# Low parts of 26 weight slabs moved from GpSimd to VectorE in a three-layer forward pass

## The chip, the cores and the metric

One core of one Trainium2 chip runs the whole program in one launch. The metric is the device time of one execution in microseconds (us); a kernel is compared by the median of its runs. The profile is that of one execution.

## The reference

256 tokens of width 1024 go through three blocks, all in float32. Cut to what matters:

```
def first_block(x, ...):                     # two layers
    for layer in range(2):
        xn = rms_norm(x, norm_mix[layer])
        x = x + (even_mixer if layer == 0 else odd_mixer)(xn, ...)
        x = x + square(relu(rms_norm(x, norm_mlp[layer]) @ w1)) @ w2     # 1024 -> 4096 -> 1024
    return rms_norm(x, norm_final)

def second_block(x, mem, ...):               # one layer
    proj = rms_norm(x) @ w_in                # 12 + 12 slabs of 256 columns
    xa, ga, qm, km, vm, qx, g_logits = split(proj)
    xa  = causal_dwconv(xa, 4 taps)
    y_a = rg_lru(xa, ...) * gelu(ga)         # gates: xa @ w_a, xa @ w_x per head, then a scan
    y_b = moba_attention(qm, km, vm)         # causal, with ALiBi slopes
    y_c = memory_cross_attention(qx, mem)
    merged = sum(sigmoid(g_logits)[n] * (y[n] @ w_branch[n]) for n in range(3))
    x = x + merged @ w_out
    h = rms_norm(x)
    x = x + (gelu(causal_dwconv(h @ w_gate, 3 taps)) * (h @ w_up)) @ w_down
    return rms_norm(x)
```

## The kernel before

Each product is made in three matmuls of a lower precision: a weight W is split into a high part `whi` (W rounded) and a low part `wlo` = W - `whi`, and so is the activation (`XH` and `XL`, `HH` and `HL`, `OH` and `OL`, `GH` and `GL`). TensorE adds high x high, low x high and high x low (line 498, `product`).

**Slabs.** `weight_plan` lists the weights as 192 slabs in the order of use, nearly all of 128 x 2048 elements (1 MB). SyncE loads slab n into one of five `raw` buffers (line 2069) when slab n - 5 has been used. ScalarE makes the high part (`high`, line 918), into one of three `whi` buffers, so it waits until TensorE has finished the slab three before. The low part is one subtraction, `wlo = raw - whi`, which waits for the high part; it is VectorE's (`low`, line 1300) or GpSimd's (`low`, line 1952). `pooled(n)` says which, and each engine goes over all slabs and skips those of the other. The numbers of the slabs that matter here: 18 to 33 `w1` and 34 to 49 `w2` of the first MLP, 86 to 89 `od_o` (the output of the second mixer), 90 to 105 `w1` and 106 to 121 `w2` of the second MLP, 122 to 133 `in2` (the third mixer's inputs), 134 to 151 twelve `gate` and six `branch` slabs in the order of `BLEND`, 152 to 155 `out2`, then `fg` and `fu` in turn.

**Order of work.** Each engine has its own program, written out by hand, and works in its order; semaphores tie them. On every engine `ahead(n)` stands where slab n is used and makes the part of slab n + 2. So a low part that VectorE makes stands in its queue in front of what it does with the product of slab n: `scaled` (line 1727) copies it out of PSUM with the norm's factor, `onto` (line 1417) and `onto_natural` (line 1424) add it to the residual `XT`, `down` (lines 1434 and 1436) does so at the end of an MLP.

**The stages of the change.** After a residual add, ScalarE makes `XH` (line 950) and VectorE `XL` (line 1334), both from SBUF; TensorE's next slab takes them chunk by chunk. GpSimd adds up the squares of the norm (line 1962). In the third mixer the first slabs feed a convolution on VectorE, `conv` (lines 1751 and 1755), and its result the LRU gates on TensorE, `lru_gate` (line 819), which stands behind slabs 126 and 127. When the LRU's scan (line 1785) is done, GpSimd loads the ALiBi distances over the gates' buffer (line 2033) and makes each head's bias (`slope`, line 2041), which the maxima of the attention need (line 1368). A step of the attention then has maxima on VectorE, exponentials on ScalarE (line 980), normalizing on VectorE (line 1383), transposes on TensorE (line 608), copies, values (line 635); between the steps stand the gate and branch slabs. `branch` multiplies by the gates and adds (lines 1833 and 1835), ScalarE and VectorE split the sum into `GH` (line 1214) and `GL` (line 1839), and `out2` takes it.

Of the kernel before, what the change touches and what calls it, by code (L numbers as in the profile page):

```python
# [265 lines left out]
def build(nc, A, out):  # L266
    with ExitStack() as ctx:
# [62 lines left out]
        plan = weight_plan(A)  # L330
# [46 lines left out]

        def pooled(n):

            name = plan[n][0]  # L380
            if name == "w1":
                return plan[n - 3][0] != "w1"
            if name == "branch":
                return sum(p[0] == "branch" for p in plan[:n]) > 1
            return name in ("out2", "in2", "fg")

        def ahead_of(n):

# [903 lines left out]
        def vector(dve):  # L1292
            once = Once(dve)

            def low(n):
                if not split(n) or pooled(n):
                    return
                once.wait_ge(*at(("raw", n)))
                once.wait_ge(*at(("whi", n)))
                dve.tensor_tensor(wlo_of(n), raw_of(n), f32(whi_of(n)), ALU.subtract).then_inc(*tell(s_wlo, ("wlo", n)))  # L1300
# [643 lines left out]
        def gpsimd(pool):  # L1944
            once = Once(pool)

            def low(n):
                if not split(n) or not pooled(n):
                    return
                once.wait_ge(*at(("raw", n)))  # L1950
                once.wait_ge(*at(("whi", n)))
                pool.tensor_tensor(wlo_of(n), raw_of(n), f32(whi_of(n)), ALU.subtract).then_inc(*tell(s_pool_wlo, ("wlo", n)))  # L1952
# [216 lines left out]
```

## Time and profile before

| | us |
|---|---|
| median of 3 runs (1332.22 to 1334.56) | 1334.36 |
| profiled execution | 1332.44 |
| its span, first to last instruction | 1330.6 |
| TensorE busy | 1265.6 |
| VectorE busy | 834.4 |
| ScalarE busy | 621.2 |
| GpSimd busy | 263.9 |

The mean granted clock of TensorE is 0.980. In the rows, PE is TensorE (PEld its weight loads), DVE VectorE, ACT ScalarE, POOL GpSimd; L918 is line 918. A row of a timeline has the start in us from the span's start, the time in us, engine, line, operation, output<-inputs, shapes and the number of instructions in the row; in brackets stands how long the engine was idle before it and what released it.

### The profile page before, as it was taken

Reading aid. Unit: us, or ns where it says so; the run is one execution under the profiler, and the core shown is the slowest. Engines: PE = TensorE matmul, PEld = TensorE weight load, DVE = VectorE, ACT = ScalarE, POOL = GpSimd, SP = SyncE. Lnnn points to the kernel's source line nnn. Section 1 sums busy time; section 2 is a strip of 40 time slices with the busy share of each in tenths; the row PEclk is TensorE's granted clock in tenths of the full one; section 3 lists DMA queues with packets and bytes.
Section 4 is the critical chain, followed back from the end, with each engine's and each line's share of the span. In section 5 each row is a group of like instructions: output and inputs, shape, how many; then the busy total and the mean of one; then the engine's idle time right before and its main releaser. Section 6 shows DMA issues by size and latency. Waiting matters only on the chain.

```text
span 1330.6 us, 23858 instructions
## 1 busy us (share of the span) xinstructions
PE 1265.6 (95%) x10309; PEld 1219.8 (92%) x10309; DVE 834.4 (63%) x1108; ACT 621.2 (47%) x761; POOL 263.9 (20%) x103
## 2 busy tenths in 40 slices
PE   7989999999999999998789999989999898999997
PEld 7967889999999999997689999989989888999997
DVE  6667556655565666666756655584777676555653
ACT  5554455544345445444355543435366445444431
POOL 2300130000012111110230000376211364433000
PEclk9999989999999999999989999999999998999998
DMA  9532345555566554544246555643543344555550
GB/s 253 171 127 88 104 137 182 190 188 179 176 224 200 183 179 156 189 156 131 65 127 190 189 176 177 196 159 127 174 149 127 127 159 135 183 190 188 176 176 32
DMA packets 194710, 213.99 MB, mean 161 GB/s; under 512 B 5235, under 2 KB 182718, under 8 KB 194606
## 3 DMA queue, kind: packets, MB, share of 16 engines
q1 hardware_dynamic: 189518, 204.93, 47.7%
q10 hardware_dynamic: 4896, 7.08, 1.8%
q8 instruction: 81, 1.33, 0.4%
q0 software_dynamic: 192, 0.46, 0.1%
q14 instruction: 23, 0.19, 0.0%
HBM read 205.11 MB, written 1.05 MB: 155 GB/s over the span
## 4 chain that ended last, share of the span: by engine, by line
PE 74%; DVE 9%; ACT 7%; issue 5%; POOL 1%; DMA 1%; ACTq 0%; DVEq 0%; POOLq 0%
PE ps L498 67%; ACT whi L918 3%; PE ps L600 2%; PE ps L635 2%; PE ps L608 1%; DVE XL L1334 1%; DVE BIG L1755 1%; ACT SN L980 1%; POOL wlo L1952 1%; DVE XT L1424 1%; DVE XT L1417 1%; DVE BIG L1835 1%; DVE SN L1368 1%; DVE BIG L1751 1%; ACT XH L950 1%
## 5 line engine op out<-in xcount | busy, mean ns | idle before, releaser
L498 PE MATMUL ps<-XH,whi 128*128 128x256 f32 x1704 | 489.0, 288 | 9.3 <-ACT XH L950 9.3
L1300 DVE TENSOR_TENSOR wlo<-raw,whi 128x2048 fp32r<-128x2048 f32 (+1 forms) x151 | 352.6, 2336 | 231.2 <-ACT whi L918 231.0
L498 PE MATMUL ps<-XL,whi 128*128 128x256 f32 x1704 | 485.1, 286 | 2.3 <-DVE XL L1334 1.6
L498 PE MATMUL ps<-XH,wlo 128*128 128x256 f32 x1704 | 483.3, 285 | 0.0
L918 ACT ACTIVATE whi<-raw 128x2048 fp32r<-128x2048 f32 (+1 forms) x189 | 359.5, 1903 | 182.9 <-PE ps L498 156.3
L498 PEld LDWEIGHTS ps<-XH,whi 128*128 128x128 f32 x1704 | 329.7, 194 | 15.4 <-ACT XH L950 11.5
L498 PEld LDWEIGHTS ps<-XL,whi 128*128 128x128 f32 x1704 | 329.2, 194 | 4.3 <-DVE XL L1334 2.9
L498 PEld LDWEIGHTS ps<-XH,wlo 128*128 128x128 f32 x1704 | 329.8, 194 | 0.2
L1952 POOL TENSOR_TENSOR wlo<-raw,whi 128x2048 fp32r<-128x2048 f32 x38 | 176.3, 4645 | 484.6 <-ACT whi L918 484.6
L498 PE MATMUL ps<-HH,whi 128*128 128x256 f32 x832 | 229.5, 283 | 0.0
L498 PE MATMUL ps<-HL,whi 128*128 128x256 f32 x832 | 229.3, 283 | 0.0
L498 PE MATMUL ps<-HH,wlo 128*128 128x256 f32 x800 | 226.5, 283 | 2.3 <-POOL wlo L1952 2.3
L498 PEld LDWEIGHTS ps<-HH,whi 128*128 128x128 f32 x832 | 157.5, 192 | 0.0
L498 PEld LDWEIGHTS ps<-HL,whi 128*128 128x128 f32 x832 | 157.5, 192 | 0.0
L498 PEld LDWEIGHTS ps<-HH,wlo 128*128 128x128 f32 x800 | 153.6, 192 | 2.5 <-POOL wlo L1952 2.5
L2013 POOL TENSOR_TENSOR TB<-TB,BIG 128x512 f32<-128x512 f32 x24 | 42.0, 1751 | 384.1 <-DMA TB<-TA 384.1
L980 ACT ACTIVATE SN<-SN,stat 128x512 f32<-128x512 f32 (+2 forms) x64 | 38.4, 600 | 141.8 <-DVE stat L1368 141.7
L498 PE MATMUL ps<-whi,XH 128*128 128x256 f32 x256 | 73.1, 285 | 0.0
L498 PE MATMUL ps<-whi,XL 128*128 128x256 f32 x256 | 72.4, 283 | 0.0
L498 PE MATMUL ps<-wlo,XH 128*128 128x256 f32 x256 | 72.4, 283 | 0.0
L608 PE MATMUL ps<-ident,SN 128*128 128x128 f32 x232 | 38.6, 290 | 20.5 <-DVE SN L1383 20.4
L498 PE MATMUL ps<-OH,whi 128*128 128x256 f32 x192 | 56.1, 292 | 1.6 <-ACT SN L980 1.6
(224 smaller groups left out, 1512.3 us busy)
## 6 DMA issues: line engine op xcount, KB each, us to landing
raw<-in_mlp_w_dram SPq DMA_DIRECT2D x64, 1024.0 KB, 5.3
raw<-in_od_w_in_dram SPq DMA_DIRECT2D x36, 1024.0 KB, 5.3
raw<-in_w_in_dram SPq DMA_DIRECT2D x24, 1024.0 KB, 5.2
raw<-in_w_ffn_gate_dram SPq DMA_DIRECT2D x12, 1024.0 KB, 5.1
raw<-in_w_ffn_up_dram SPq DMA_DIRECT2D x12, 1024.0 KB, 5.1
raw<-in_w_ffn_down_dram SPq DMA_DIRECT2D x12, 1024.0 KB, 5.1
raw<-in_ev_w_in_dram SPq DMA_DIRECT2D x6, 1024.0 KB, 12.1
TB<-TA ACTq DMA_DIRECT2D x96, 64.0 KB, 4.2
```

What stands on the lines that cost most here:

```text
L498: m = pe.matmul(to, l[c][a], r[c][b], start=first and k == 0, stop=last and k == 3 * n - 1)
L600: m = pe.matmul(banks[u][:, lo:hi], l, r, start=start, stop=stop)
L608: m = pe.transpose(b[:, to:to + P], SN[:, u % 3, of:of + P], ident[:, :])
L635: m = pe.matmul(b[p0:p0 + n, a:z], v, PT[:, u % 3, lo:hi], start=start, stop=stop)
L918: act.activation(whi_of(n), raw_of(n), ACT.Copy, scale=1.0).then_inc(*tell(s_whi, ("whi", n)))
L950: act.activation(XH[:, c, :], XT[:, c, :], ACT.Copy, scale=g).then_inc(*tell(s_xhi, ("xhi", stage, c)))
L980: m = act.activation(SN[:, u % 3, lo:hi], src[:, lo:hi], ACT.Exp, bias=stat[:, u % 3, k:k + 1], scale=-1.0 if biased else 1.0, accum_out=s ...
L1300: dve.tensor_tensor(wlo_of(n), raw_of(n), f32(whi_of(n)), ALU.subtract).then_inc(*tell(s_wlo, ("wlo", n)))
L1334: dve.scalar_tensor_tensor(out=XL[:, c, :], in0=XT[:, c, :], scalar=g, in1=f32(XH[:, c, :]), op0=ALU.mult, op1=ALU.subtract).then_inc(*tel ...
L1368: m = dve.tensor_tensor_reduce(out=SN[:, u % 3, lo:hi], in0=b[:, lo:hi], in1=bias(lo), scale=-0.125 if kind == DIL else -1.0, scalar=3e38, ...
L1952: pool.tensor_tensor(wlo_of(n), raw_of(n), f32(whi_of(n)), ALU.subtract).then_inc(*tell(s_pool_wlo, ("wlo", n)))
L2013: pool.tensor_tensor(z, z, twice(RP[:, S:512]), ALU.mult).then_inc(*tell(s_pool, ("sine", k)))
```

## The change

`pooled(n)` gave GpSimd the low parts of 38 slabs: the first three `w1` slabs of either MLP (18 to 20, 90 to 92), all twelve `in2` slabs, the last four of the six `branch` slabs (146, 149, 150, 151), the four `out2` slabs and the twelve `fg` slabs. Now it gives it the twelve `fg` slabs alone. The other 26 are made by VectorE, with the same subtraction, each at the place in its queue where `ahead` stands. Nothing else is changed.

```diff
         def pooled(n):
 
-            name = plan[n][0]
-            if name == "w1":
-                return plan[n - 3][0] != "w1"
-            if name == "branch":
-                return sum(p[0] == "branch" for p in plan[:n]) > 1
-            return name in ("out2", "in2", "fg")
+            return plan[n][0] == "fg"
 
         def ahead_of(n):
```

## Rows read from the trace of the kernel before

**Rows 1.** The page's engine table: busy us, share of the span, instructions.

```profile
PE 1265.6 (95%) x10309; PEld 1219.8 (92%) x10309; DVE 834.4 (63%) x1108; ACT 621.2 (47%) x761; POOL 263.9 (20%) x103
```

**Rows 2.** Windows: length, busy us by engine, granted clock, DMA share, GB/s.

```profile
869.00:910.00 41.00, 36.27 (x280) 32.70 (x280) 34.08 (x36) 14.26 (x15) 25.25 (x6) 0.92 0.38 123
...
950.00:1046.00 96.00, 92.15 (x764) 87.60 (x760) 67.91 (x116) 53.06 (x83) 18.38 (x11) 1.00 0.44 145
...
1090.00:1118.00 28.00, 21.82 (x155) 21.04 (x156) 14.66 (x17) 12.13 (x17) 18.77 (x7) 0.88 0.36 116
```

**Rows 3.** The low parts by line: ns min/median/max, first and last start, forms.

```profile
L1952 POOL TENSOR_TENSOR wlo<-raw,whi x38: 4543/4622/5073, 161.3 to 1228.8; 128x2048 fp32r<-128x2048 f32 x38
...
L1300 DVE TENSOR_TENSOR wlo<-raw,whi x151: 2265/2292/4321, 16.5 to 1306.0; 128x2048 fp32r<-128x2048 f32 x150, 128x1280 fp32r<-128x1280 f32 x1
```

**Rows 4.** Two lines of VectorE, the second with an input in PSUM.

```profile
L1334 DVE SCALAR_TENSOR_TENSOR XL<-XT,V,XH x32: 472/480/4901, 9.0 to 1111.5; 128x256 fp32r<-128x256 f32 x32
...
L1727 DVE SCALAR_TENSOR_TENSOR BIG<-ps,RS x22: 678/683/693, 874.2 to 1058.4; 128x512 f32<-128x512 f32 x22
```

**Rows 5.** Timeline of GpSimd at the mixer's input.

```profile
873.81 14.22 POOL L1952 TENSOR_TENSOR wlo<-raw,whi 128x2048 fp32r<-128x2048 f32 x3 [3.22 <-ACT whi L918]
```

**Rows 6.** Timeline of VectorE there.

```profile
856.55 3.62 DVE L1436 TENSOR_TENSOR XT<-XT,TA 128x256 f32<-128x256 f32 x1
...
875.70 3.08 DVE L1751 TENSOR_SCALAR BIG<-BIG,V 128x256 f32<-128x256 f32 x1
878.81 10.01 DVE L1755 SCALAR_TENSOR_TENSOR BIG<-BIG,V 128x255 f32<-128x255 f32 x3
...
895.94 1.52 DVE L1755 SCALAR_TENSOR_TENSOR BIG<-BIG,V 128x255 f32<-128x255 f32 x3
```

**Rows 7.** Timelines ahead of the first MLP, GpSimd and VectorE.

```profile
168.75 4.61 POOL L1952 TENSOR_TENSOR wlo<-raw,whi 128x2048 fp32r<-128x2048 f32 x1 [2.86 <-ACT whi L918]
...
169.79 4.25 DVE L1334 SCALAR_TENSOR_TENSOR XL<-XT,V,XH 128x256 fp32r<-128x256 f32 x2 [0.65 <-ACT XH L950]
```

**Rows 8.** Timelines ahead of the second MLP, VectorE and GpSimd.

```profile
647.83 1.14 DVE L1424 TENSOR_TENSOR XT<-XT,ps 128x256 f32<-128x256 f32 x2 [0.46 <-PE ps L498]
...
651.30 2.56 DVE L1383 TENSOR_SCALAR SN<-SN,stat 128x512 f32<-128x512 f32 x1
...
663.62 3.95 DVE L1334 SCALAR_TENSOR_TENSOR XL<-XT,V,XH 128x256 fp32r<-128x256 f32 x2 [0.65 <-ACT XH L950]
...
648.98 4.59 POOL L1952 TENSOR_TENSOR wlo<-raw,whi 128x2048 fp32r<-128x2048 f32 x1 [35.92 <-ACT whi L918]
```

**Rows 9.** The LRU gates by line, columns as in rows 3.

```profile
L819 PE MATMUL ps<-BIG,SN x32: 376/376/685, 892.3 to 908.9; 64*64 64x256 f32 x32
```

**Rows 10.** The chain that ended last, behind the first gate: start, us, what.

```profile
900.51 6.87 PE ps L498 x48
907.39 1.87 PE ps L819 x16
909.26 5.96 PE ps L498 x48
```

**Rows 11.** The same chain ahead of the attention.

```profile
951.74 4.17 DMA BIG<-in_c_alibi_dram
```

**Rows 12.** Timelines of the mixer's end, VectorE, TensorE and ScalarE.

```profile
1042.63 4.81 DVE L1835 TENSOR_TENSOR BIG<-BIG,TB 128x512 f32<-128x512 f32 x1
...
1073.93 0.68 DVE L1833 TENSOR_TENSOR TB<-ps,BIG 128x512 f32<-128x512 f32 x1
...
1076.72 0.68 DVE L1833 TENSOR_TENSOR TB<-ps,BIG 128x512 f32<-128x512 f32 x1
...
1085.87 5.73 DVE L1417 TENSOR_TENSOR XT<-XT,ps 128x512 f32<-128x512 f32 x8
...
1049.64 1.09 PE L608 MATMUL ps<-ident,SN 128*128 128x128 f32 x4 [3.99 <-DVE SN L1383]
...
1110.53 0.91 ACT L950 ACTIVATE XH<-XT,V 128x256 fp32r<-128x256 f32 x2 [0.70 <-DVE XT L1417]
```

## The prediction

> **What bounds the kernel now.** I read the page's engine table first: TensorE is busy for 1265.6 of 1330.6 us [rows 1]. At most 65 us can be won, and only where TensorE waits. So I read the windows of the stages that the 38 GpSimd low parts stand in. TensorE idles for 4.7 us of 869 to 910, 3.9 us of 950 to 1046 and 6.2 us of 1090 to 1118, and its granted clock is 0.92 and 0.88 in the first and the last, 1.00 between [rows 2]. The MLPs and the GLU behind have no such gaps.
>
> Then I read the low parts by line. One takes 4.62 us on GpSimd and 2.29 us on VectorE [rows 3]. GpSimd's own speed is hardly waited for. What matters is what its instruction does to VectorE: an XL of L1334 takes 0.48 us as a rule and up to 4.90 us, while L1727, which reads PSUM, stays within 678 to 693 ns [rows 4]. In the timelines GpSimd works from 873.81 to 888.03 without a pause [rows 5], and in that time VectorE's convolution, all in SBUF, takes 3.08 us for an instruction of 0.40 and 10.01 us for three that need 1.52 later [rows 6]. I read this as: of the two engines' instructions that have all their data in SBUF, one runs at a time, and the other engine's waits for its end.
>
> **First MLP (slabs 18 to 20): 0.9 us won.** On VectorE low 18 runs while it would idle, and low 20 while it waits for the norm's sums. Low 19 stands in front of the last residual adds. Its high part ends at 168.6, just before GpSimd starts at 168.75 [rows 7], so VectorE holds it from 168.65 to 170.9, then add 0.7, high half 0.5 behind it, two XL 0.9: done at 173.1. Now the two XL are blocked until 174.0 [rows 7].
>
> **Second MLP (90 to 92): 0.4 us lost.** Low 90 comes in front of the adds of `od_o`: until 651.2 (high part done by 648.9, when GpSimd starts), where four adds now begin at 647.8. With 0.8 us of waits absorbed and the 2.1 us block at 651.30 gone (2.56 against 0.49), the last heads run 0.8 us later. Low 91 delays the residual adds by 3.1 us more and saves the 3.95 - 0.88 = 3.1 us block and some hand-over, about 0.4 back [rows 8]. Low 92 lies in the wait for sums. Bounds: 0.4 won to 1.0 lost.
>
> **Mixer input (122 to 133): 0.6 + 7.3 us won.** One of the MLP's last two `down` adds is blocked by low 123 now (3.62 us at 856.55 instead of 0.42 [rows 6]); low 123 on VectorE delays it by 1.4 us, less than that. So TensorE's 0.6 us wait for the last XH goes. Then I place VectorE's queue from the factors' end (873.9): low 125 2.2, slab 0.6, two convolutions of 1.9 (0.40 + 1.52, as at 895.94) [rows 6], low 126, slab, two convolutions. The four are ready at 887.9. TensorE reaches the first LRU gate at 892.3 - 0.6 = 891.7, so it doesn't wait. Before, the gate's 16 matmuls lasted from 892.3 [rows 9] to 900.5, and the second gate's, with nothing to wait for, 1.87 us; the slab between them took 6.87 us instead of 5.9 [rows 10]. That is 8.2 - 1.9 = 6.3 us and 1.0 us: 7.3. The other low parts (127 to 133) come 1.7 us or more ahead of TensorE in the same placing, the tightest being 133 (ready 928.8, wanted 930.5). Between them VectorE does the ratios unblocked.
>
> **Attention of the mixer: 3.5 us won.** GpSimd starts the alibi load at 951.74, when the scan is done; it lands 4.2 us later, and the first slope follows [rows 11]. In my placing the scan is done at 939.9: the load starts 11.5 us earlier, and with it the chain of maxima, exponentials, high part, low part. TensorE is only 7.9 us earlier, so its waits here, 3.85 us of which 0.35 belong to the wait that ends at 1049.64, go [rows 2, 12]. Low 146 costs nothing: ScalarE's gates and their two table loads last longer than it.
>
> **Branches and output slab (149 to 155): 5.2 us won.** I count from the end of the last gate slab before the last transposes, 1045.65 (1049.64 - 3.99); call it A. The 3.99 us wait goes: it stands behind a branch add that took 4.81 instead of 0.69 [rows 12]. Then TensorE: transposes and values 1.1, slabs 148 and 149 11.7, values 0.7, four slabs of 5.8. Slab 153 ends at A + 36.7 and frees the buffer of high part 156, which is done at A + 38.7; GpSimd, which keeps `fg`, starts low 156 at A + 38.8. VectorE: low 152 at A + 16.1 (ScalarE must first copy the last attention output) to 18.3; two merges of 2.79 (1073.93 to 1076.72) [rows 12] to 23.9; 1.1 of waiting for high part 153; low 153 to 27.3; two merges to 32.9; 1.1 of waiting; low 154 from 34.0 to 36.2; four residual adds of 0.72 (8 in 5.73) [rows 12]; low 155 at A + 39.1. GpSimd is 0.3 us ahead. So low 155 is held until 43.4 and ends at 45.7, where TensorE wanted it at 42.4. Behind it: four adds 2.9, two residual blocks of 2.1, ScalarE's high part and low 157 to 56.9, one block more, one add. The last high half starts at A + 59.7. Now it starts at 1110.53, which is A + 64.9 [rows 12]: 5.2 us. The FFN and all after it are TensorE without gaps, so this stays won to the end.
>
> **Rule against row.** The Trainium skill's page Perfetto Trace Analysis, section Optimizing Scalar/DVE Operations, says that shifting work between VectorE and GpSimd may not help, since they share a read port. By that rule alone the 26 low parts would only change who waits, and the sum would be near 0 (1332.4). The rows say that the one keeps the other out for 4.62 us and the other needs 2.29 us for the same work [rows 3], so I keep the sum. The page SBUF — State Buffer, section SBUF: two separate sides, says that the pair belongs to whichever instruction starts first, for all of it; the blocked XL [rows 4, 7] agree, and by that rule too 0.3 us decide on 4 us at slab 155.
>
> **Sum.** -0.9 + 0.4 - 0.6 - 7.3 - 3.5 - 5.2 = -17.1 us. VectorE gets 26 x 2.29 = 59.5 us more, GpSimd 120 us less. The profiled execution took 1332.4 us, so 1315.3; the median of the runs is 1.9 us above it, by which it is 1317.3. I say 1316.5.
>
> **Rivals.**
> - VectorE first at slab 155 (0.27): 0.3 us in a chain of twenty instructions is little. Then low 155 ends at A + 41.4, GpSimd waits, and the end of the tail comes 4.1 us earlier: 21.2 us won, 1311.2 to 1313.1.
> - The alibi load held (0.12): it is issued from GpSimd, just as VectorE runs low 136. If its start or its writing waits for VectorE's low parts, all that follows slips: two low parts are 4.6 us, 1320; at worst all of the 11.5 us, 1326.8. Against it: low 136 stood behind the scan before too, and the load took 4.17 us [rows 11]. The skill's page SBUF — State Buffer has a warning of this kind on loads from GpSimd's queue; no row here shows one.
> - Slower (0.05): VectorE's long instructions are not GpSimd's doing. Then the blocks stay and low parts come on top, in its queue ahead of what TensorE waits for: 124 to 127 before the convolutions (9.2 us), 152 to 155 before the residual (9.2), 19, 90 and 91 (6.9, less 4 hidden): about 1354. It decides once XL and convolution keep over half of their extra time with GpSimd idle. Against it: 0.48 us is their median [rows 4].
> - No change (0.06): TensorE's waits turn up elsewhere, in loads of weights or a lower clock, and 1332 to 1336 stays. Against it: the DMA share is 0.38 and 0.44 where the waits are [rows 2].
> - The forecast has 0.50.
>
> Chances: faster 0.50 + 0.27 + 0.12 = 0.89, same 0.06, slower 0.05, with 0.2% (2.7 us) as the bound, about what a measurement of this kernel can tell. The range goes from 1309 (VectorE first, the second MLP at its better bound) to 1327 (the alibi load at worst), and leaves out the last two cases.
>
> **What would show it.** L1952 has 12 instructions and L1300 177; nearly all L1334, L1751 and L1755 take 0.4 to 0.5 us; the LRU gate has no wait on L1755; the alibi load starts 11 to 12 us earlier; low 155 takes either 2.3 us or over 6. I am wrong if VectorE's durations don't fall, if a wait on L1300 of more than 4 us appears at TensorE, or if the mixer's attention starts early and TensorE isn't earlier at its end.

## The result and the profile after

| | before | after |
|---|---|---|
| median of 4 runs each, us | 1334.46 (1332.22 to 1336.17) | 1315.44 (1314.61 to 1317.58) |
| ratio, 95% interval | | 0.9861 (0.9841 to 0.9880) |
| profiled execution, us | 1332.44 | 1317.58 |
| its span, us | 1330.6 | 1315.8 |

The kernel is 19 us faster on the medians; the two profiled executions lie 14.9 us apart. Lines of the changed kernel have numbers smaller by 5: L1300 is now L1295, L498 L493, L819 L814, L1334 L1329.

The page's engine table of the changed kernel. TensorE's busy time is 2.5 us below what it was [rows 1]; VectorE took over 26 low parts, 59.5 us of work, and its busy time rose by 7 us only. The rest had been time in which its instructions stood still.

```profile
PE 1263.1 (96%) x10309; PEld 1221.5 (93%) x10309; DVE 841.5 (64%) x1134; ACT 621.6 (47%) x761; POOL 144.6 (11%) x77
```

The changed kernel by line, columns as in [rows 3]. Twelve low parts are left on GpSimd. No XL takes over 486 ns (up to 4901 before [rows 4]), and the convolution's two lines take 0.40 and 0.48 us everywhere. One low part on VectorE takes 6.5 us.

```profile
L1947 POOL TENSOR_TENSOR wlo<-raw,whi x12: 4562/4626/4630, 1075.0 to 1214.9; 128x2048 fp32r<-128x2048 f32 x12
...
L1295 DVE TENSOR_TENSOR wlo<-raw,whi x177: 2265/2292/6535, 16.3 to 1292.1; 128x2048 fp32r<-128x2048 f32 x176, 128x1280 fp32r<-128x1280 f32 x1
...
L1329 DVE SCALAR_TENSOR_TENSOR XL<-XT,V,XH x32: 475/480/486, 9.2 to 1096.8; 128x256 fp32r<-128x256 f32 x32
...
L1746 DVE TENSOR_SCALAR BIG<-BIG,V x4: 402/405/409, 880.0 to 888.5; 128x256 f32<-128x256 f32 x4
...
L1750 DVE SCALAR_TENSOR_TENSOR BIG<-BIG,V x12: 482/483/485, 880.5 to 889.9; 128x255 f32<-128x255 f32 x4, 128x254 f32<-128x254 f32 x4, 128x253 f32<-128x253 f32 x4
```

Windows of the changed kernel, columns as in [rows 2]. The first row, the end of the second mixer, is taken up further below. The mixer's input and its attention have no gap left at TensorE (4.7 and 3.9 us before [rows 2]). The residual of the tail, the last row, has 7.8 us of gaps, and a mean granted clock of 0.82, a mixture of the two levels, 1.2 and 2.4 GHz, behind TensorE's waits.

```profile
625.00:660.00 35.00, 25.79 (x216) 22.51 (x216) 26.33 (x59) 12.36 (x24) 0.00 (x0) 0.87 0.20 61
869.00:912.00 43.00, 43.00 (x355) 40.95 (x355) 33.81 (x44) 18.92 (x23) 0.00 (x0) 1.00 0.47 152
944.00:1040.00 96.00, 96.00 (x798) 91.84 (x797) 65.98 (x124) 55.48 (x85) 9.48 (x8) 1.00 0.47 153
1075.00:1104.00 29.00, 21.20 (x142) 20.11 (x141) 18.14 (x20) 10.69 (x16) 13.01 (x5) 0.82 0.32 105
```

The timeline of VectorE at the mixer's input: low 125 and the convolution behind it. Three instructions that took 10.01 us [rows 6] take 1.52.

```profile
877.23 2.28 DVE L1295 TENSOR_TENSOR wlo<-raw,whi 128x2048 fp32r<-128x2048 f32 x1
879.42 0.68 DVE L1722 SCALAR_TENSOR_TENSOR BIG<-ps,RS 128x512 f32<-128x512 f32 x1
880.03 0.40 DVE L1746 TENSOR_SCALAR BIG<-BIG,V 128x256 f32<-128x256 f32 x1
880.46 1.52 DVE L1750 SCALAR_TENSOR_TENSOR BIG<-BIG,V 128x255 f32<-128x255 f32 x3
```

The chain of the changed kernel there. Both LRU gates take 1.9 us, the slab between them 5.9, as the forecast had it.

```profile
894.05 1.88 PE ps L814 x16
895.93 5.94 PE ps L493 x48
901.87 1.87 PE ps L814 x16
903.74 8.34 PE ps L493 x68
```

Timelines of the changed kernel: GpSimd's alibi load and first slope, then low 155 and 156 (VectorE, GpSimd) and TensorE's waits behind them. The load starts 9.8 us earlier than at [rows 11]. GpSimd starts low 156 at 1075.03, VectorE reaches low 155 at 1075.26, 0.23 us too late; 6.54 is 4.4 us of standing and 2.2 of work. The two starts lie 0.23 to 0.24 us apart in each of the five traces with this order of work.

```profile
941.90 0.58 POOL L2028 DMA_DIRECT2D BIG<-in_c_alibi_dram  x1 [77.13 <-DVE BIG L1780]
944.83 3.46 POOL L2036 TENSOR_SCALAR TB<-BIG 128x384 f32<-128x384 f32 x3 [2.35 <-DMA BIG<-in_c_alibi_dram]
...
1075.26 6.54 DVE L1295 TENSOR_TENSOR wlo<-raw,whi 128x2048 fp32r<-128x2048 f32 x1
...
1075.03 4.62 POOL L1947 TENSOR_TENSOR wlo<-raw,whi 128x2048 fp32r<-128x2048 f32 x1 [91.68 <-ACT whi L913]
...
1081.85 0.39 PE L493 MATMUL ps<-HH,wlo 128*128 128x256 f32 x1 [2.60 <-DVE wlo L1295]
1094.27 0.58 PE L493 MATMUL ps<-XH,whi 128*128 128x256 f32 x1 [4.88 <-ACT XH L945]
1096.39 0.58 PE L493 MATMUL ps<-XH,whi 128*128 128x256 f32 x1 [0.31 <-ACT XH L945]
```

### The profile page after: what moved, and what is told of

Read it like the earlier page. It is cut to its first block, busy times and chain, and to the rows that moved or that the text cites. A ratio compares the mean times of both kernels' runs of the same rounds, so it can differ in the third digit from the quotient of the medians.

```text
span 1315.8 us, 23857 instructions
## 1 busy us (share of the span) xinstructions
PE 1263.1 (96%) x10309; PEld 1221.5 (93%) x10309; DVE 841.5 (64%) x1134; ACT 621.6 (47%) x761; POOL 144.6 (11%) x77
## 3 DMA queue, kind: packets, MB, share of 16 engines
HBM read 205.11 MB, written 1.05 MB: 157 GB/s over the span
## 4 chain that ended last, share of the span: by engine, by line
PE 84%; DVE 6%; ACT 3%; issue 3%; DMA 0%; ACTq 0%; POOL 0%; DVEq 0%
PE ps L493 76%; PE ps L595 2%; PE ps L630 2%; PE ps L603 2%; ACT whi L913 2%; DVE XT L1419 1%; DVE XT L1412 1%; DVE wlo L1295 1%; DVE XL L1329 1%; DVE SN L1363 1%; PE ps L529 1%; ACT XH L945 0%; ACT SN L975 0%; DMA TB<-TA 0%; PE ps L814 0%
## 5 line engine op out<-in xcount | busy, mean ns | idle before, releaser
L1295 DVE TENSOR_TENSOR wlo<-raw,whi 128x2048 fp32r<-128x2048 f32 (+1 forms) x177 | 417.1, 2357 | 260.5 <-ACT whi L913 260.3
L493 PE MATMUL ps<-XH,whi 128*128 128x256 f32 x1704 | 489.0, 288 | 10.4 <-ACT XH L945 10.4
L493 PE MATMUL ps<-XL,whi 128*128 128x256 f32 x1704 | 485.5, 286 | 0.8 <-DVE XL L1336 0.4
L493 PE MATMUL ps<-XH,wlo 128*128 128x256 f32 x1704 | 483.9, 285 | 0.0
L493 PEld LDWEIGHTS ps<-XH,whi 128*128 128x128 f32 x1704 | 330.2, 194 | 15.4 <-ACT XH L945 12.2
L493 PEld LDWEIGHTS ps<-XL,whi 128*128 128x128 f32 x1704 | 329.9, 194 | 2.6 <-DVE XL L1329 1.2
L493 PEld LDWEIGHTS ps<-XH,wlo 128*128 128x128 f32 x1704 | 330.3, 194 | 0.1
L493 PE MATMUL ps<-HH,whi 128*128 128x256 f32 x832 | 229.6, 284 | 0.2 <-DVE XT L1412 0.2
L493 PE MATMUL ps<-HL,whi 128*128 128x256 f32 x832 | 229.3, 283 | 0.0
L493 PE MATMUL ps<-HH,wlo 128*128 128x256 f32 x800 | 226.5, 283 | 2.6 <-DVE wlo L1295 2.6
L493 PEld LDWEIGHTS ps<-HH,whi 128*128 128x128 f32 x832 | 157.5, 192 | 0.4 <-DVE XT L1412 0.4
L493 PEld LDWEIGHTS ps<-HL,whi 128*128 128x128 f32 x832 | 157.5, 192 | 0.0
L493 PEld LDWEIGHTS ps<-HH,wlo 128*128 128x128 f32 x800 | 153.6, 192 | 2.8 <-DVE wlo L1295 2.8
L1947 POOL TENSOR_TENSOR wlo<-raw,whi 128x2048 fp32r<-128x2048 f32 x12 | 55.4, 4620 | 161.8 <-ACT whi L913 161.8
L493 PE MATMUL ps<-whi,XH 128*128 128x256 f32 x256 | 73.1, 285 | 0.0
L493 PE MATMUL ps<-whi,XL 128*128 128x256 f32 x256 | 72.4, 283 | 0.0
L493 PE MATMUL ps<-wlo,XH 128*128 128x256 f32 x256 | 72.4, 283 | 0.0
L493 PE MATMUL ps<-OH,whi 128*128 128x256 f32 x192 | 57.3, 299 | 2.8 <-ACT SN L975 2.0
L493 PE MATMUL ps<-OL,whi 128*128 128x256 f32 x192 | 55.4, 288 | 0.0
```

The source lines that it names most:

```text
L493: m = pe.matmul(to, l[c][a], r[c][b], start=first and k == 0, stop=last and k == 3 * n - 1)
```

## The experiments

The theory, **blocks**: of VectorE's and GpSimd's instructions with all data in SBUF one runs at a time, so GpSimd's low part of 4.62 us holds up what VectorE has next. The rival, **late weights**: TensorE waited for the low parts themselves, which GpSimd makes slowly. Each group below was compared on one chip with common runs of the kernel before (its median is given).

### One part of the change at a time (before: 1335.78 us, 22 runs)

**Mixer input alone**

```diff
-            return name in ("out2", "in2", "fg")
+            return name in ("out2", "fg")          # the tests for w1 and branch stay
```

> Only the twelve in2 slabs (122 to 133) on VectorE, the rest as before. Theory of the blocks (a GpSimd instruction on SBUF keeps VectorE's instructions on SBUF waiting, and their lateness is what TensorE waits for): the LRU gate's waits go and the alibi load starts 11 to 12 us earlier, so 0.6 + 7.3 + 3.5 = 11.4 us faster than before, about 1323; the 4 us wait behind the branch add at the mixer's end stays. Rival, the late weights (GpSimd's 4.6 us make the low parts late): no wait of TensorE on GpSimd's low part stands there, so no change, 1334.

1319.02 us (4 runs), ratio 0.9875 (0.9856 to 0.9895): 16.8 us won where 11.4 was forecast, most of the whole. The LRU gates wait no more. The profiled execution is 13.0 us below that of before, and one wait of the attention is left, TensorE's timeline in this kernel:

```profile
1036.47 0.88 PE L608 MATMUL ps<-ident,SN 128*128 128x128 f32 x4 [2.11 <-DVE SN L1383]
```

It took 3.99 us before [rows 12]: with the chain of the attention earlier, half of that wait goes without the branch slabs being moved. The forecast had left it whole; the other part of the 5 us too much is not accounted for.

**Branch and output slabs alone**

```diff
-            if name == "branch":
-                return sum(p[0] == "branch" for p in plan[:n]) > 1
-            return name in ("out2", "in2", "fg")
+            return name in ("in2", "fg")           # the test for w1 stays
```

> Only the four branch slabs (146, 149 to 151) and the four out2 slabs on VectorE. Blocks: 5.2 us faster than before, about 1329, the 4 us wait before the last transposes gone. Late weights: only the 2.3 us wait on GpSimd's low part of slab 154 goes, about 1332.

1328.76 us (11 runs), ratio 0.9958 (0.9941 to 0.9974): 7.0 us won on the medians, 3.5 to 7.9 by the interval. That holds the 5.2 us of blocks and not the 2.3 us of late weights. TensorE's timeline still shows the LRU gate's waits on the convolution, with in2's low parts on GpSimd:

```profile
895.14 0.65 PE L817 MATMUL ps<-BIG,SN 64*64 64x256 f32 x4 [2.14 <-DVE BIG L1753]
897.70 1.12 PE L817 MATMUL ps<-BIG,SN 64*64 64x256 f32 x4 [1.92 <-DVE BIG L1753]
```

**MLP slabs alone**

```diff
-            if name == "w1":
-                return plan[n - 3][0] != "w1"      # the rest stays
```

> Only the six w1 slabs (18 to 20, 90 to 92) on VectorE. Prediction's terms: 0.9 won and 0.4 lost, 1334. If what the profile after shows at the second MLP (3.5 us later than the same stretch of before) is the work of low 90 and 91 in VectorE's queue, 2.5 to 3 us slower, about 1337; if it is the granted clock of that one execution, 1334. Late weights: 1334.

1335.50 us (12 runs), ratio 0.9998 (0.9987 to 1.0008): nothing. Six of the 26 moves are worth nothing together, which is near the sum of the forecast's two terms (-0.9 and +0.4); the trace of this kernel says more on them below. The three parts add up to 24.1 us, the whole won 19.0 above and 17.5 below. About 1.9 us of the last wait of the attention count in the first two parts both. The rest of the difference is not accounted for; the collision of the low parts 155 and 156 is no reason, since the branch and output slabs alone have it too (low 155 starts at 1086.26, 0.23 us behind low 156, and takes 6.54 us).

**The blocks put back.** The changed kernel, with GpSimd subtracting constants into idle tiles when the high part of each in2 slab is done. Nothing waits for these results.

```diff
                 if not pooled(n):
+                    if plan[n][0] == "in2":
+                        once.wait_ge(*at(("whi", n)))
+                        if n > 123:
+                            once.wait_ge(*at(("dummy", n - 2)))
+                        pool.tensor_tensor(<OH or OL, idle here, 128x2048>,
+                                           <ident, broadcast>, <ones, broadcast>, ALU.subtract)
+                            .then_inc(*tell(s_pool, ("dummy", n)))
                     return
```

> The changed kernel, and GpSimd does twelve subtractions of the same size (128 x 2048, constants into the idle OH and OL) at the times of its former low parts of the in2 slabs; nothing waits for their results. Blocks: the waits of TensorE at the LRU gate are back, and longer than in the kernel before by about 4.5 us, since VectorE has two low parts more in that queue: 11 to 16 us slower than the changed kernel, 1327 to 1332. Late weights: VectorE's low parts are as early as in the changed kernel and so is the end, 1315.

1350.32 us (6 runs), ratio 1.0104 (1.0087 to 1.0121): 14.5 us above the kernel before and 34 to 35 above the medians of the changed kernel, for twelve instructions on an engine that had nothing to do. Late weights fall here: GpSimd makes none of these weights, and the time was to stay at 1315. The sign is that of blocks; the size and the place were wrong. The LRU gate does not wait in this trace; TensorE waits 3.93 us for XH and 3.04, 11.03 and 5.61 us for low parts that VectorE makes late. I had priced the convolution only. Timelines of this kernel (VectorE, GpSimd, TensorE):

```profile
887.15 5.99 DVE L1295 TENSOR_TENSOR wlo<-raw,whi 128x2048 fp32r<-128x2048 f32 x1
...
897.76 9.84 DVE L1750 SCALAR_TENSOR_TENSOR BIG<-BIG,V 128x255 f32<-128x255 f32 x3
...
890.92 6.65 POOL L1950 TENSOR_TENSOR OH<-ident,ones 128x2048 fp32r<-128x2048 f32 x1
...
893.19 0.39 PE L493 MATMUL ps<-XH,wlo 128*128 128x256 f32 x1 [3.04 <-DVE wlo L1295]
...
911.74 0.58 PE L493 MATMUL ps<-XH,wlo 128*128 128x256 f32 x1 [11.03 <-DVE wlo L1295]
...
957.76 0.58 PE L493 MATMUL ps<-wlo,XH 128*128 128x256 f32 x1 [5.61 <-DVE wlo L1295]
```

With long instructions on both engines each pays for the other: low parts on VectorE take up to 6.76 us, GpSimd's instruction takes 6.65 us behind one of them, and three instructions of the convolution take 9.84 again. So now TensorE does wait for low parts, those of VectorE.

### Order, load and length (before: 1334.21 us, 11 runs)

**The changed kernel again**

> The changed kernel once more, beside the others of this call: 1315.4, 19 to 20 us faster than before.

1316.74 us (5 runs), ratio 0.9855 (0.9835 to 0.9875): 17.5 us below the kernel before, a little less than said.

**Low 155 first.** The changed kernel, with VectorE's low 155 ahead of the residual adds of slab 152:

```diff
             for k in range(2):
                 ahead(OUT2 + k)
+            for k in range(2):
                 for j in range(4):
                     onto(OUT2 + k, j, j)
```

> The changed kernel with low 155 ahead of the residual adds of slab 152 in VectorE's queue, so that it starts 2.9 us earlier, before GpSimd's low 156 can. Blocks (who starts first holds the other off): low 155 takes 2.3 us, TensorE's 2.6 us wait for it goes, the residual chain ends 4.1 us earlier: 1311.3. Rival, the residual chain hangs on something else there: TensorE waits as long, but on XH, 1315.4.

1310.50 us (4 runs), ratio 0.9821 (0.9802 to 0.9840): 6.2 us below the changed kernel on the medians, and its slowest run is faster than the fastest of the other. VectorE's timeline there, then TensorE's:

```profile
1069.84 2.28 DVE L1295 TENSOR_TENSOR wlo<-raw,whi 128x2048 fp32r<-128x2048 f32 x1
1072.04 6.45 DVE L1412 TENSOR_TENSOR XT<-XT,ps 128x512 f32<-128x512 f32 x9
...
1072.78 0.39 PE L493 MATMUL ps<-HH,whi 128*128 128x256 f32 x1 [2.39 <-DVE XT L1412]
1087.86 0.39 PE L493 MATMUL ps<-XH,whi 128*128 128x256 f32 x1 [0.39 <-ACT XH L945]
```

Low 155 takes 2.28 us and the nine adds, which read PSUM, run beside GpSimd's low 156 (1072.48 to 1077.08) at their usual 0.72 us. TensorE's four waits of the tail of over 0.1 us, 7.98 us, become three of 3.54. The 2.60 us wait for low 155 does not simply go, as expected: TensorE now waits 2.39 us for the adds, which stand behind low 155. What goes is most of the 4.88 us wait for XH, of which 0.39 is left.

**The alibi load held back.** The changed kernel, with a wait of GpSimd for the product of the second gate slab ahead of the load:

```diff
             once.wait_ge(*at("lru h"))
+            once.wait_ge(*at(("product", "slab", BLENDS + 1)))
             pool.dma_start(alibi, A["c_alibi"])
```

> The changed kernel, with GpSimd's alibi load held until TensorE has finished gate slab 135, some 9 us later than in the changed kernel and at the time it had before. The prediction's step (attention runs on the VectorE and ScalarE chain that the load starts): TensorE waits for the normalized scores again, 5 to 8 us slower than the changed kernel, about 1322. Rival, TensorE's slabs bound the attention and the load's time is covered: 1315.4.

1325.21 us (6 runs), ratio 0.9938 (0.9917 to 0.9959): 8.5 us above the changed kernel, where 5 to 8 was forecast. Timelines, GpSimd and TensorE:

```profile
947.06 0.58 POOL L2029 DMA_DIRECT2D BIG<-in_c_alibi_dram  x1 [86.88 <-PE ps L493]
952.52 3.46 POOL L2037 TENSOR_SCALAR TB<-BIG 128x384 f32<-128x384 f32 x3 [4.88 <-DMA BIG<-in_c_alibi_dram]
...
961.87 0.90 PE L603 MATMUL ps<-ident,SN 128*128 128x128 f32 x3 [8.78 <-DVE SN L1378]
```

The load is issued 5.2 us later than in the changed kernel, not 9, and takes 2.5 us longer to land. A slope that comes 7.7 us later is one wait of 8.78 us. The time of this load is what the attention hangs on.

**Shorter holds.** The kernel before, all 38 low parts on GpSimd still, each in four instructions of 128x512:

```diff
-                pool.tensor_tensor(wlo_of(n), raw_of(n), f32(whi_of(n)), ALU.subtract).then_inc(*tell(s_pool_wlo, ("wlo", n)))
+                w, r, h = wlo_of(n), raw_of(n), f32(whi_of(n))
+                for s in <the four quarters of the slab>:
+                    m = pool.tensor_tensor(w[s], r[s], h[s], ALU.subtract)
+                m.then_inc(*tell(s_pool_wlo, ("wlo", n)))
```

> The kernel before, all 38 low parts on GpSimd as there, each as four instructions of a quarter (128 x 512) in place of one. Blocks: VectorE gets in after 1.2 us at most, not 4.6, so its blocks at the XL, the branch adds and the normalizing shrink to a quarter, those of the convolution by less, because GpSimd's next quarter follows at once: 3 to 9 us faster than before, about 1329. Late weights: the low parts take 4.6 us or more as before, no gain or slower, 1335 to 1337.

1313.72 us (6 runs), ratio 0.9849 (0.9826 to 0.9872): as much as the change itself. The theory's side is right, its size too low by 15 us. The quarters by line, GpSimd's timeline at the mixer's input, VectorE's convolution beside it, and TensorE at the LRU gate:

```profile
L1956 POOL TENSOR_TENSOR wlo<-raw,whi x152: 1259/1297/1747, 159.6 to 1210.9; 128x512 fp32r<-128x512 f32 x152
...
870.69 22.22 POOL L1956 TENSOR_TENSOR wlo<-raw,whi 128x512 fp32r<-128x512 f32 x16 [3.02 <-ACT whi L918]
...
872.36 1.23 DVE L1751 TENSOR_SCALAR BIG<-BIG,V 128x256 f32<-128x256 f32 x1
873.63 4.26 DVE L1755 SCALAR_TENSOR_TENSOR BIG<-BIG,V 128x255 f32<-128x255 f32 x3
...
893.76 1.04 PE L819 MATMUL ps<-BIG,SN 64*64 64x256 f32 x4 [3.32 <-DVE BIG L1755]
```

The low parts are made no faster (four quarters take 5.2 us, one whole 4.62), so late weights fall a second time. VectorE gets one instruction in after each quarter: 1.42 us each where it was 3.3 [rows 6]. GpSimd is busier than before, 288.7 us, and the kernel is 20 us faster.

### The collision at the tail, and the length again (before: 1334.05 us, 11 runs)

**All low parts on VectorE**, with low 155 first:

```diff
-            return plan[n][0] == "fg"
+            return False
```

> VectorE makes all low parts, the twelve of fg too, with low 155 ahead of the residual adds of slab 152; GpSimd only adds up squares. By the theory (one engine's all-SBUF instruction keeps the other's out), GpSimd can hold nothing up any more, but low 156 now stands in VectorE's queue in the residual chain, where it costs its own 2.3 us: 1312 to 1314, 2 us above the kernel with the order changed alone (1310.5). If VectorE becomes the bound in the FFN (twelve times 2.3 us more in some 185 us, of which it is busy for 111): 1320 or more.

1313.19 us (4 runs), ratio 0.9843 (0.9822 to 0.9864): the time that the theory gave, 2.7 us above low 155 first alone, though the two intervals overlap. The twelve more low parts do not make VectorE the bound (861.9 us busy); the residual chain pays for low 156 in one longer wait at TensorE, 3.69 us where it was 0.39:

```profile
1088.20 0.58 PE L493 MATMUL ps<-XH,whi 128*128 128x256 f32 x1 [3.69 <-ACT XH L945]
```

**Low 155 first, fg's low parts in quarters.** The diffs of the two kernels above, together.

> The kernel with the order changed (low 155 ahead of the residual adds of slab 152), with GpSimd's twelve low parts of fg made in four instructions each. By the theory nothing that TensorE waits for is held by GpSimd any more, so the quarters have nothing left to win: 1310.5 as without them, within 1.5 us. If quarters win by something other than shorter holds (GpSimd itself faster, for instance): 1307 or less.

1312.97 us (5 runs), ratio 0.9827 (0.9805 to 0.9849). The median is 2.5 us above the 1310.5, outside the 1.5 us that I gave; against the ratio of 0.9821 of low 155 first alone the intervals overlap, so no difference is shown. Quarters win nothing where nothing that TensorE waits for is held.

**Halves.** The kernel before, with each low part in two instructions of 128x1024.

> The kernel before, with each of GpSimd's low parts made in two instructions of 128x1024 instead of one of 128x2048. If the loss goes with the length of one hold (4.6 us whole, 1.26 us in quarters, about 2.4 us in halves), about half to two thirds of what the quarters won is won here: 1321 to 1325. If any gap between GpSimd's instructions is enough, since VectorE has one waiting instruction at a time: 1314 to 1317, like the quarters.

1322.78 us (6 runs), ratio 0.9914 (0.9889 to 0.9939): 11 of the quarters' 20 us. The loss goes with the length of a hold; a gap alone is not enough. The line of the low parts, then TensorE's waits at the LRU gate and at the end of the attention:

```profile
L1956 POOL TENSOR_TENSOR wlo<-raw,whi x76: 2343/2407/2867, 158.8 to 1223.0; 128x1024 fp32r<-128x1024 f32 x76
...
895.00 0.65 PE L819 MATMUL ps<-BIG,SN 64*64 64x256 f32 x4 [1.35 <-DVE BIG L1755]
...
1045.08 1.09 PE L608 MATMUL ps<-ident,SN 128*128 128x128 f32 x4 [2.35 <-DVE SN L1383]
```

## Why the prediction was right

The steps between marks of the two profiled executions, after against before:

| mark | after - before, us | step, measured | step, forecast |
|---|---|---|---|
| first LRU gate starts (894.0, 892.3) | +1.7 | +1.7 | -1.1 |
| slab behind the second gate starts (903.74, 909.26) | -5.5 | -7.2 | -7.3 |
| end of the last gate slab, A (1036.22, 1045.65) | -9.4 | -3.9 | -3.5 |
| last high half at TensorE (1096.39, 1111.09) | -14.7 | -5.3 | -5.2 |
| end of the span (1315.8, 1330.6) | -14.8 | -0.1 | 0 |

- **The mechanism** held where TensorE hung on it: taken away in one part (mixer input, output), put back without the weights (34 to 35 us lost), and made shorter (halves, quarters). By the Trainium skill, page SBUF — State Buffer, section SBUF: two separate sides, whichever instruction starts first keeps the pair for all of it; the 0.23 us at low 155 and the quarters agree, the slopes (below) do not. The page Perfetto Trace Analysis of the Trainium skill, section Optimizing Scalar/DVE Operations, says that moving work between the two might not help, since they share a read port. That they get in each other's way is what the rows show; that the sum would be near 0 for it is not: the move gave 19 us.
- **Its wording was too wide.** What the traces show held are VectorE's `tensor_tensor`, `scalar_tensor_tensor` and `tensor_scalar` with all data in SBUF. A reciprocal, all in SBUF too, is not held: in the kernel before, the one at 924.57 lies inside GpSimd's first low part (924.44 to 929.07) and takes 3.35 us, as the one at 934.41 does with GpSimd idle (VectorE, then GpSimd):

```profile
924.57 3.35 DVE L1770 RECIPROCAL TA<-TA 128x512 f32<-128x512 f32 x1
...
934.41 3.35 DVE L1770 RECIPROCAL TA<-TA 128x512 f32<-128x512 f32 x1
...
924.44 9.65 POOL L1952 TENSOR_TENSOR wlo<-raw,whi 128x2048 fp32r<-128x2048 f32 x2 [0.20 <-ACT whi L918]
```

Nor does every GpSimd instruction hold to its end: beside a slope, a `tensor_scalar` of 1.20 us, VectorE's first normalizing takes 0.55 us for 0.29 and the second its usual 0.34, and both end before the slope does (five times in the kernel before; the profile's spans of GpSimd are rough). On this form the rows do not bear out the rule that the Trainium skill gives, and the rows decide. So look at the pair of instructions, not only at where their data lie.

- **Mixer input and attention.** The gates run without a wait, the alibi load comes 9.8 us earlier and TensorE has no gap from 944 to 1040. I had the load 11.5 us earlier; the difference is the 2.8 us lost ahead of the gates (below), less 1 us; so the 11 to 12 us that was to show it did not come. From issue to landing it took 2.9 us, by the view of DMA issues, where [rows 11] had 4.2. The rival with the load held did not come: low 136 ran on VectorE from 941.52 to 943.8, over the issue, and the load was there at 944.8.
- **Tail.** GpSimd was ahead by 0.23 us where I had 0.3, low 155 stood, TensorE waited 2.60 us for it, and the step came out as 5.3 for 5.2. A margin of 0.3 us at the end of a chain of twenty placed instructions came out partly by luck, though in the five traces it comes out the same. The rival, VectorE first, was priced at 4.1 us less and a median of 1313.1; the experiment that puts low 155 first won 6.2 us.
- **MLPs: the mis-sized term.** -0.9 + 0.4 - 0.6 was to be -1.1 at the first gate and was +1.7: -0.8 stood there ahead of the first moved instruction, +0.2 came from the first MLP, +3.5 from the second and -1.1 behind it (rounded). Ahead of the first MLP the last XH came 0.9 us earlier as placed, but TensorE's next 30 matmuls took 6.34 us in place of 5.20, at a granted clock of 0.57 in place of 0.72, so that the 0.9 us were lost again.
- **The second MLP** is the term that failed, and the largest miss. The same 360 matmuls of TensorE, from 619.3 to 680.8 us before and from 618.6 to 683.6 after, took 61.6 and 65.0 us. Of these 3.5 us, 1.5 were lost before VectorE reached low 90, the first instruction moved there; the granted clock of 625 to 660 was 0.87, and 0.98 before. The prediction said that the MLPs have no gaps like those of its three windows, and it shows none for the stage in which low 90 stands. That stage has 9.8 us of them, so that there a late VectorE makes TensorE late (the window in the kernel before, columns as in [rows 2]):

```profile
625.00:660.00 35.00, 25.21 (x243) 22.01 (x239) 27.38 (x59) 12.13 (x24) 4.59 (x1) 0.98 0.19 61
```

This is not the chance of one execution: those 360 matmuls take 64.0 to 65.0 us in all eight traces with these slabs on VectorE, and 61.5 to 63.1 in the four with them on GpSimd whole or in halves (quarters: 60.4). Against it stand the 12 runs with the MLP slabs alone moved, which are no slower (0.9998, at the most 1.1 us by the interval). What gives the loss back in them, and what part of it is the clock, stays open.

- **The total** agrees better than its parts. The profiled execution was to be 1315.3 and was 1317.6: the 2.3 us are the first mark's 2.8, less 0.4 of the attention and 0.1 of the tail. The median was to be 1316.5 and was 1315.4; the sum itself gave 1317.3, and the prediction has no reason for the 0.8 us between, so the last microsecond is luck. The two parts taken alone won 16.8 and 7.0 us on the medians where 11.4 and 5.2 were forecast.

## What to carry to other kernels

When VectorE and GpSimd both work on data in SBUF, look at the longest duration of VectorE's short instructions, not at GpSimd's busy share: a median of 0.48 us with a maximum of 4.90 points to a hold, the two timelines side by side show it, and its price is paid by whoever waits for VectorE. Such work can be moved to VectorE, if it has time in that stage, or left on GpSimd in short pieces, which here gave as much (1313.7 against 1316.7). Where one long instruction stays, look which other stands next to it in time, and change their order: one line of order was worth 6.2 us, and that version, 1310.5 us, has the lowest median here.

## What was not expected of the hardware

- **Pieces take turns.** GpSimd had no pause in 22.22 us of quarters, and VectorE still got its waiting instruction in after each of them. I had priced a shorter hold as a share of the old loss (3 to 9 us), and it gave 20.
- **Both engines pay.** Twelve subtractions whose results nobody used raised GpSimd's busy time by 62 us, VectorE's by 46 (887.4 for 841.5), and made the kernel 34 to 35 us slower than the changed one.
- **Waits cost clock as well.** In the tail of the kernel with low 155 first, the granted clock of 1075 to 1104 was 0.95, in the changed kernel 0.82: TensorE's waits there differ by 4.4 us, the two kernels' medians by 6.2. The same 300 matmuls of the tail take 42.9 and 48.7 us in the two traces, 5.8 us apart, so some 1.4 us beyond the waits are slower matmuls.
- **One load, two landing times.** The alibi load, 192 KB from GpSimd's queue, was waited for 2.1 to 2.4 us after its issue in nine profiled executions, and 3.7 to 5.1 us in four (the kernel before, the branch and output slabs alone, the MLP slabs alone, and the load held back). In these four it was issued between 947 and 955 us, but the halves issued it at 949.45 and waited 2.1. A low part of VectorE is not the cause: one ran over the issue in twelve of the thirteen, and none in the load held back, which waited 4.9. What goes with it is the weights' queue: in the four, 0.89 to 1.05 MB of weights moved between issue and landing, in the nine 0.39 MB or less. No run tried that by itself.
